# Layer 0 of a two-layer hybrid decoder step, rewritten as one loop over its 28 projection units with the attention and the decode inside

## The reference

```
z = rmsnorm(x, norm_g) @ w_in            # 1024 -> 3584 columns = 28 tiles of 128
qa, ka, va, qb, kb, vb, gb = split(z)    # 4 tiles each; qa, ka, qb, kb are turned by rope
oa = block-sparse attention(qa, ka, va)  # prompt: causal over 256 tokens, 8 heads x 64
                                         # decode: 1024 cached tokens, best 3 of 4 blocks of 256, plus own
ob = retention(qb, kb, vb, state)        # prompt in chunks; decode: state = g * state + k v
x += concat(oa, headnorm(ob) * silu(gb)) @ w_out     # 8 tiles of 128
```

## Time and profile before

| | us |
|---|---|
| median of 3 runs (lowest, highest) | 959.08 (958.39, 960.77) |
| span of the profiled execution | 959.2 |
| PE, DVE, ACT, POOL busy in it | 883.4, 622.1, 420.1, 257.4 |
| loop over the units | 23.8 to 148 |
| prompt attention and retention | 148 to 202 |
| decode softmax | 202 to 216.9 |
| value pages | 216.9 to 298.5 |
| first matmul of the output projection | 302.4 |

### The profile page before, as it was taken

How to read it: one execution, slowest core, us unless ns; L and a number is a source line. 1 busy time by engine, 2 the same in 40 slices (tenths; PEclk the granted TensorE clock), 3 DMA queues, 4 the chain that set the end, 5 groups by cost and what they waited for, 6 DMA issues and landing times.

```text
span 959.2 us, 16875 instructions
## 1 busy us (share of the span) xinstructions
PE 883.4 (92%) x6145; PEld 761.0 (79%) x6145; DVE 622.1 (65%) x943; ACT 420.1 (44%) x695; POOL 257.4 (27%) x226
## 2 busy tenths in 40 slices
PE   2999894969999999999999999969969999999996
PEld 1988783742325999999999999857648999999995
DVE  3689988660032798888556656565476888887442
ACT  4434333341011565555545433564334655555442
POOL 6154767710100332232001000161221332222010
PEclk9999996588999999999999999975597999999997
DMA  9837675335565555554556667403353566653631
GB/s 275 284 129 242 199 260 183 128 94 160 192 220 175 176 177 175 178 184 129 172 177 192 191 187 216 161 10 100 88 155 93 171 192 188 188 157 121 183 119 46
DMA packets 154406, 159.83 MB, mean 167 GB/s; under 512 B 11793, under 2 KB 136349, under 8 KB 154335
## 3 DMA queue, kind: packets, MB, share of 16 engines
q1 hardware_dynamic: 145520, 151.09, 50.6%
q10 hardware_dynamic: 7966, 6.33, 2.2%
q0 software_dynamic: 864, 1.68, 0.7%
HBM read 150.76 MB, written 8.50 MB: 166 GB/s over the span
## 4 chain that ended last, share of the span: by engine, by line
PE 81%; DVE 11%; ACT 4%; issue 2%; DMA 2%; ACTq 0%; POOL 0%; SPq 0%; DVEq 0%
PE bank L1396 20%; PE bank L1397 20%; PE bank L1398 20%; PE bank L1604 6%; DVE w_lo L921 3%; DVE sc_all L973 2%; PE bank L1773 1%; PE bank L1726 1%; DMA z<-in_c_out_norm_g 1%; PE bank L1485 1%; PE bank L1600 1%; PE bank L1566 1%; PE bank L1748 1%; PE bank L1737 1%; DVE z L968 1%
## 5 line engine op out<-in xcount | busy, mean ns | idle before, releaser
L530 ACT ACTIVATE w_hi<-w_raw 128x1024 fp32r<-128x1024 f32 (+2 forms) x230 | 227.9, 993 | 297.8 <-PE bank L1398 294.5
L921 DVE TENSOR_TENSOR w_lo<-w_raw,w_hi 128x1024 fp32r<-128x1024 f32 (+2 forms) x230 | 296.1, 1289 | 83.6 <-ACT w_hi L530 83.4
L1396 PE MATMUL bank<-actB_hi,w_hi 128*128 128x264 f32 x704 | 200.1, 284 | 0.0
L1397 PE MATMUL bank<-actB_lo,w_hi 128*128 128x264 f32 x704 | 199.5, 283 | 0.0
L1398 PE MATMUL bank<-actB_hi,w_lo 128*128 128x264 f32 x704 | 199.3, 283 | 0.0
L1396 PE MATMUL bank<-actA_hi,w_hi 128*128 128x264 f32 x624 | 184.8, 296 | 5.8 <-DVE w_lo L921 2.9
L1397 PE MATMUL bank<-actA_lo,w_hi 128*128 128x264 f32 x624 | 180.1, 289 | 0.0
L1398 PE MATMUL bank<-actA_hi,w_lo 128*128 128x264 f32 x624 | 179.8, 288 | 0.0
L1397 PEld LDWEIGHTS bank<-actB_lo,w_hi 128*128 128x128 f32 x704 | 132.6, 188 | 0.1
L1396 PEld LDWEIGHTS bank<-actB_hi,w_hi 128*128 128x128 f32 x704 | 132.6, 188 | 0.1
L1398 PEld LDWEIGHTS bank<-actB_hi,w_lo 128*128 128x128 f32 x704 | 132.0, 187 | 0.0
(11 more groups left out here) (326 smaller groups left out, 1191.2 us busy)
## 6 DMA issues: line engine op xcount, KB each, us to landing
w_raw<-in_ffn_w SPq DMA_DIRECT2D x44, 1024.0 KB, 5.3
kv<-in_cache_k SPq DMA_DIRECT2D x64, 256.0 KB, 3.0
kv<-in_cache_v SPq DMA_DIRECT2D x64, 256.0 KB, 3.1
w_raw<-in_c_w_in SPq DMA_DIRECT2D x16, 1024.0 KB, 5.6
w_raw<-in_ab_w_in SPq DMA_DIRECT2D x14, 1024.0 KB, 5.4
w_raw<-in_ffn_w SPq DMA_DIRECT2D x16, 768.0 KB, 4.5
w_raw<-in_ffn_w SPq DMA_DIRECT2D x16, 640.0 KB, 4.1
w_raw<-in_ab_w_out SPq DMA_DIRECT2D x4, 1024.0 KB, 5.7
```

The lines of the kernel that those rows point to most:

```text
L530: A(whi[u % RING][:, 0:nk, :], raw[u // 2 % RING][:, 0:nk, P * (u % 2):P * (u % 2) + P], ACT.Copy).then_inc(sem("hi_ready"), 1)
L921: V.tensor_tensor(wlo[u % RING][:, 0:nk, :], raw[u // 2 % RING][:, 0:nk, P * (u % 2):P * (u % 2) + P], whi[u % RING][:, 0:nk, :].bitcast(F ...
L1396: M(bank[b][:, 0:T], hi[:, k, :], src[0][:, k0 + k, :], start=first and k == 0, stop=False)
L1397: M(bank[b][:, 0:T], hi[:, k, :], src[1][:, k0 + k, :], start=False, stop=False)
```

## The change

Only layer 0 and the loads that belong to it are rewritten. Its parts:

1. **Start.** x is scaled by its reciprocal root as token rows, before it is turned: ACT sums squares along the rows (three instructions), the root is taken of 3 columns, the scaled rows go through PE, and ACT and DVE split what comes out (`act_hi`, `act_lo`). The squares' matmuls on PE and the factor `rstd` behind every unit are gone. The unscaled x is turned too, half of it before the loop, half behind units 1 and 2. The constants are loaded in three pieces, x first.
2. **Rope.** DVE makes both products (cosine and sine) of a roped tile in one instruction of 528 elements straight from PSUM; PE turns the sine part and adds the cosine part in one PSUM bank (two products of 264 columns); ACT takes the sum out. Unroped tiles are taken out by ACT alone. POOL has no part in it any more.
3. **The loop.** Prompt attention of the eight heads stands inside it, one head for every second unit from 9 on; so do all key products (six page buffers in place of four, and a table `K_SUMS` of how many sums are done by which unit), the decode softmax of sequences 0 to 3 (`samp_stats(0)` and what follows, units 17 to 20), and the first two retention scores.
4. **Softmax of the decode** works on 32 rows (four sequences) twice, reads the scores in PSUM, and divides by way of a diagonal matrix on PE. Prompt scores are masked and their maximum taken in one DVE instruction per part (`tensor_tensor_reduce`).
5. **Values.** Pages are taken page position by page position for four sequences: `v_quad` multiplies four pages, one of each sequence, into rows 0, 32, 64 and 96 of one bank. A second list of page numbers in that order is loaded (`pgv`). A pair of buffers is refilled when its quad is done; the first six value buffers wait for key sums 27 to 32. Retention heads, states and their norms stand between the quads.
6. **State.** The decode state is loaded by SP behind the third quad's pages, into z tiles that are free by then, after waits for the last prompt scores.

The core of the diff:

```
+PAGES = [("k", j) for j in range(32)] + [("v", n // 2) for n in range(32)]
+KSLOTS = 6
+K_SUMS = {6: 1, 7: 3, 8: 4, 9: 6, 10: 8, 11: 9, 12: 11, 13: 12, 14: 14, 15: 16, 16: 17, 17: 19, 18: 20, 19: 22, 20: 24,
+          21: 25, 22: 27, 23: 28, 24: 30, 25: 32}
...
-            for j in range(32):
-
-                page_pair(j, cache_v, (sem("k_reduced"), 29 + j) if j < 4 else (sem("v_used"), j - 3))
...
+            w_in(17)
+            for n in range(3):
+                v_pages(n)
+            sp.wait_ge(sem("attn_s"), H)
+            sp.wait_ge(sem("jobs_in"), JOBS.index(("t", "va", 2)) + 1)
+            for c in range(4):
+                sp.dma_start(s0[c], state_ret[0, :, 2 * c:2 * c + 2].rearrange("b q d e -> (q d) b e")).then_inc(sem("s0_landed"), 16)
+            for n in range(3, 16):
+                v_pages(n)
...
+            pool.wait_ge(sem("x_landed0"), 16)
+            pool.wait_ge(sem("x_landed1"), 16)
...
-            for u in range(28):
-                if u in ROPED:
...
-                    G.tensor_tensor(rmk[r % 2][:, 0:T], z0[:, u, :], cos, ALU.mult).then_inc(sem("cos_prod"), 1)
-                if u >= 8:
-                    k_mult(u - 8)
-            for j in range(20, 32):
+            for j in range(32):
                 k_mult(j)
...
+                V.tensor_tensor(cossin[r % 2], bank[u % 2][:, 0:T].unsqueeze(1).to_broadcast([P, 2, T]),
+                                cst[:, C_COS:C_COS + 2 * T].rearrange("p (a n) -> p a n", a=2), ALU.mult
+                                ).then_inc(sem("cos_sin"), 1)
...
+            def v_quad(n):
+
+                q, g = n // 8, n % 8
+                out = [bank[V_BANKS[q]][32 * i:32 * i + H, :] for i in range(4)]
...
+                for i in range(4):
+                    b = 4 * q + i
+                    ins = M(out[i], pts[:, g, 8 * b:8 * b + 8], kv[(at + i // 2) % KSLOTS][:, i % 2, :], start=False, stop=g == NPAGE - 1)
+                ins.then_inc(sem("v_used"), 1)
```

More of the change, by code:

```diff
@@ L289, in k_pages @@
[L289 to L303, removed]
-                if n >= 10:
-                    k_pages(2 * n - 16)
-                    k_pages(2 * n - 15)
@@ new lines, in act_lo @@
+            def act_lo(k):
+                dve.wait_ge(sem("norm_hi"), k + 1)
+                V.scalar_tensor_tensor(actA[1][:, k, :], bank[4 + k % 4][:, 0:T], gains[:, G_AB + k:G_AB + k + 1],
+                                       actA[0][:, k, :].bitcast(F32), ALU.mult, ALU.subtract).then_inc(sem("norm_lo"), 1)
+            for k in range(4):
+                x_raw(k)
+            dve.wait_ge(sem("row_ss"), 3)
+            V.tensor_scalar(sm[:, 3:6], sm[:, 0:3], 1.0 / D, EPS, ALU.mult, ALU.add).then_inc(sem("rms_var"), 1)
@@ L1051, in _ @@
-            blocks = prow.rearrange("p (n k) -> p n k", n=NBLK)
-            gate = sm[0:64, 12:16]
-            V.tensor_reduce(sm[0:64, 16:20], blocks, AX, ALU.max)
-            step(V.tensor_reduce(gate, blocks, AX, ALU.add))
-            dve.wait_ge(sem("own_s"), 1)
-            V.tensor_copy(sm[0:64, 68:69], bank[7][0:64, 0:1]).then_inc(sem("own_in"), 1)
-            for n in range(NBLK):
-                if n:
-                    V.tensor_scalar(sm[0:64, 40 + 4 * n:40 + 5 * n], gate[:, 0:n], gate[:, n:n + 1], None, ALU.is_ge)
-                last = V.tensor_scalar(sm[0:64, 40 + 5 * n:44 + 4 * n], gate[:, n:NBLK], gate[:, n:n + 1], None, ALU.is_gt)
@@ new lines, in sum_squares, with x_turn @@
+                pe.wait_ge(sem("sq_ready"), 8 * (stage - 1) + 1)
+                M(bank[7][:, 0:T], ones[:], sq[:, 0, :], start=True, stop=True).then_inc(sem("ss_done"), 1)
+            def x_turn(k):
+                b = k if k < 4 else 6 + k % 2
+                claim(b, "x_ready", k + 1)
+                for t in range(2):
+                    TR(bank[b][:, P * t:P * t + P], x_tok[:, t, P * k:P * k + P], ident)
+                TR(bank[b][:, TP:T], xs_tok[:, P * k:P * k + P], ident[0:NB, 0:NB]).then_inc(sem("x_t"), 1)
@@ new lines, in _ @@
+            ret_state()
+            v_quad(7)
+            for c in range(4):
+                v_quad(8 + c)
+                state_update(2 * c)
+                state_update(2 * c + 1)
+            v_quad(12)
+            for c in range(4):
+                ret_o(0, c)
+            v_quad(13)
+            for c in range(4):
+                ret_o(1, c)
+            v_quad(14)
+            for c in range(4):
+                ret_squares(c)
+            v_quad(15)
+            claim(2, "mix_lo", 5)
```

880 lines of the change are left out of this document (534 added, 346 removed), and 6 rows, old and new, of the table JOBS_AFTER.

## The result

The changed kernel takes 934.5 us (median of four runs, 932.0 to 935.3) against 959.9 us in the same comparison, a ratio of 0.971 (95% interval 0.967 to 0.975). It is faster, but by 25 us and not by the 71 that I forecast; 934.5 also lies above my range. In the profiled execution (span 932.7) unit 1 starts at 25.6 us, the loop ends at 185.7 and the first matmul of the output projection stands at 275.0. What follows takes 657.7 us, as before (656.8). So all of the difference lies ahead of 275 us, and the forecast of 231 there was 44 us short: 22.7 in the loop (185.7 for 163) and 21.3 behind it (89.3 for 68).

What follows compares the result with a forecast made beforehand. It saw limits by stage: PE in the loop, a chain of small steps in attention, PE among value pages. Loop to 163 plus 68 put the output projection at 231, not 302.4: 71 us less, 888 us (8 in 10: 866 to 927).

Steps and rivals of the forecast that it cites:

- The quads pack: Value pages: four matmuls writing rows 32 apart run side by side, 0.95 us per quad.
- the rival without packing: Value pages: the four matmuls of a quad do not run together, 41 us back on PE, 923 us; chance 0.09.
- rule of strict order: Value quads: matmuls start and end in program order, so a quad takes 2.2 us and the time is about 893.
- PE's sum of the loop: Loop: units, rope, query rows, attention and small pieces sum to 132 us of PE, ending at 157.
- The norm's wait: Behind the last quads: the norm's chain, hidden before, stands in the open for 9.7 us.
- I add 5 for waits in order and let the loop end at 163: Loop: PE ends at 157, POOL and DVE at 158; a flat 5 us covers waits between engines.
- DVE's own work: Loop: splits, sums, rope pairs, scores and softmax on DVE sum to 85 us, less than its sum with POOL.
- the sum of the pair: Loop: POOL's key products and DVE's SBUF-to-SBUF steps cannot overlap, so they add to 107 us, ending at 158 with one sum.
- My rival of a slower loop: Loop: hand-overs between four engines and POOL's hold on tiny steps add 23 us, giving 911; chance 0.14.
- Then the pages bind: Behind the loop: page transfers set the pace of the value quads, 2.65 us per quad, 34.5 us for thirteen.
- for steps at the lower clock I add 4: Behind the loop: a flat 4 us for PE steps running at the lower clock.
- my 68: From the loop's end to the output projection: softmax, quads, state products, norm's chain and clock take 68 us, ending at 231.

Runs made afterwards that it cites:

- out_softmax: Changed kernel with ACT's copy of the attention output first in its unit and the first four sequences' decode softmax moved behind the loop; 915.8 us (901 to 926).
- out_early: Changed kernel with ACT's copy that frees the attention output's bank moved from last to first among a unit's steps; 922.3 us.
- short products: Changed kernel with POOL's key products cut to 16 of 1,024 elements per partition, here with ACT's attention output copy first; 914.0 us with both.
- all three together: Changed kernel with value pages from fixed places, state products spread in groups of 32, extra constant matmuls before quads 8 to 15, and a DVE mask moved; 917.0 us.
- fixed_pages: Changed kernel with value pages taken from fixed cache places, so SP reads no page numbers for them; 918.3 us.
- pe_filled: Changed kernel with extra constant matmuls ahead of PE's page waits, eight before quad 8 and three before each of quads 9 to 15; 924.4 us.
- best: Changed kernel with ACT's attention output copy first, page numbers read before the buffer wait, and state products spread; computes all; 913.1 us.

## Why the prediction was wrong

**What held.** The start: unit 1 at 25.6 for 25. The quads pack: 0.97 us for my 0.95; the rival without packing falls. The Trainium skill's rule of strict order ("TensorE: Matmul & The Clock Gate", section "The mechanism"), which I had weighed as 2.2 us per quad, does not hold as I applied it: 1.0 us at 2.4 GHz. That page's section "Measured speedup vs the span model" has 2.38 for three column groups; here four took 0.97 us against 0.87 for one, 3.6 times. PE's sum of the loop: 133.0 for 132 where the pauses are gone, and the softmax with them (its 27 units make 78.3 us, not 78.6, which changes nothing). The norm's wait: 9.5 for 9.7. The part behind: unchanged to 1 us.

**First step that failed: "I add 5 for waits in order and let the loop end at 163."** PE waited 16.4 us, and its work took 12 us more than its sum. Against out_softmax, 4.6 us of this work are units at 1.2 GHz (units 17, 20 and 25 take 5.2, 4.8 and 4.2 us for 3.2), 1.6 the attention's value products at that clock, and 4.6 the softmax's own matmuls. I had compared the engines' sums and put a flat 5 us on top, without following one unit's turn through ACT's and DVE's lists. The places were in the order of the program: a copy behind a step that waits for two other engines (8.3 us), and the softmax's statistics ahead of the split that unit 20 needs (14.8 us more, from out_early to out_softmax).

The second is not the softmax's alone. With the early copy, short products in place of the moved softmax end the loop at 165.6, nearly as early as its 162.6; this points to DVE's list, which either cure relieves. For DVE's own work from the first key product to unit 25 I had 85 us; it was busy 100 (changed kernel, 49.6 to 172.5), and the splits held beside POOL's products make the difference, 16 us. I had counted that hold in the sum of the pair, not in DVE's own, and my reading of the earlier trace rows was loose: in the time of those four products DVE had not two splits of 1.17 us but three of 3.1 to 3.4 and a rope sum, so DVE paid for most of it. Nor did POOL's products run all but gapless to 155, as I expected: from 101 us on they waited 22.5 us for key pages and 9 for a query row, and the last ended at 168.7. My rival of a slower loop had the right size (186) and part of the cause: it named the hold of POOL, which gives 6.5 us alone and 11.8 with the early copy, and the hand-over between engines, but not the copy.

**Second step: "Then the pages bind", 2.65 us per quad, and "for steps at the lower clock I add 4".** By the terms of my sum, in order: quads 0 to 3 with the softmax, 16.0 for 18; quads 4 to 7, 15.0 for 6; quads 8 to 11 with their state pairs, 20.7 for 11; quads 12 to 14, products and sums, 23.0 for 15; norm's chain, turn and split, 14.6 for 13.5; and the clock's 4 are inside these. Three things were mis-sized. SP reads eight page numbers in 2.7 us behind its wait, for two quads; with four issues of 0.52 that makes 3.5 us per quad. The landing takes 4.5 us (the median among the value pages) for 3.1. And the clock: from 221.7 to 275 it is at 1.2 GHz nearly throughout. At 2.4 GHz seven quads, four pairs, 128 products, the sums and the selections of this stretch would take about 20 us less (an estimate, 6 + 4 + 6 + 2 + 2, by their durations at either level). One cure alone gave at most 6.0 us, all three together 14.8. Two limits at nearly one level, SP's 3.5 us per quad and PE's 3.9 at 1.2 GHz, would explain it, since lifting one leaves the other; but the single gains are near the scatter, so their shares are argued and not shown.

I had read the attention stage at a mean clock of 0.62 (with two levels, three quarters of it at the lower one, not the half that I wrote) and put its price into one flat term, though the new order moves that kind of work, short steps with pauses, into the whole stretch. Of such work the Trainium skill says ("TensorE: Matmul & The Clock Gate", section "HAM oscillation — how this bites in real kernels") that a matmul burst that waits for DMA again and again pays the lower clock again and again. The trace agrees at quad 8 of the changed kernel (1.90 us behind a wait of 4.0). It goes further at the state products, where the clock falls while PE is busy, and in fixed_pages, where quad 4 takes 1.89 us with no wait ahead of it.

What stays open: the 6.5 us between 74.5 and my 68, which by the rows lie in the products at 1.2 GHz and the norm's chain; what takes the clock down where PE hardly pauses; and the varying part in layer 1.

## What to carry to other kernels

Before you add a few us for "waits in order", take one unit of the new loop and walk it through each engine's list: a wait that goes through three engines inside one unit is paid in full, and then again in the clock behind it. Where several limits lie at one level, as SP's pages, PE's clock and DVE's order did here, price them together: single edits gave up to 10 us, edits together 15 behind the loop and 20 to 23 in it. Price work at the clock that its neighbourhood will have, not at the one of the row it was read from.

## What the runs showed of the hardware

- Sixty-four rows of state products in a row (32 matmuls with 64 x 64 weights and one column each, in pe_filled) took the granted clock from 1.00 to 0.50 with PE busy all the time; groups of sixteen rows between value matmuls, in the kernel before, left it at 0.97 over that stage.
- Reading eight page numbers into SP's registers took 2.7 us: a load of 0.54 and eight steps of about 0.25, during which no page is asked for. The steps of that line (count, ns at least, median and most, first and last start):

```profile
L320 SPq FUSED_REGOPS  x128: 147/147/181, 14.8 to 237.8; - x128
L320 SPq SEQ_ASSERT  x128: 18/18/28, 15.0 to 238.0; - x128
...
L320 SPq TENSOR_LOAD <-pgv x8: 523/536/1123, 170.2 to 235.3; - x8
```
- The pause right ahead of a quad does not tell its clock: behind 2.2 us quad 4 of the changed kernel took 1.90 us and quad 6 of best 1.04; with no pause ahead of it quad 4 of fixed_pages took 1.89.
